# Sums over partitions of twelve modulation blocks, and two gate rows, by DMA and VectorE instead of by TensorE

## What is computed

```python
mod = jnp.dot(jax.nn.silu(c), w_ada) + b_ada            # c: 1 x 1024, w_ada: 1024 x 6144
shift1, scale1, gate1, shift2, scale2, gate2 = jnp.split(mod, 6, axis=-1)
h = _rmsnorm(x, norm1_w) * (1.0 + scale1) + shift1      # input of the mixer (stage 6)
x = x + gate1 * jnp.dot(merged, w_out)
h2 = _rmsnorm(x, norm2_w) * (1.0 + scale2) + shift2     # input of the last FFN (stage 7)
x = x + gate2 * ffn
```

## Time and profile before

| | |
|---|---|
| time, median of 3 runs | 1506.94 us (1505.27 to 1507.37) |
| the profiled execution | 1505.48 us |
| its span, first to last instruction | 1503.7 us |
| granted TensorE clock, mean | 0.992 |
| busy: PE / DVE / ACT / POOL | 1450.5 / 951.1 / 713.1 / 161.4 us |
| instructions: PE / DVE / ACT / POOL | 6819 / 1315 / 1034 / 260 |
| DMA | 279.15 MB, 201717 packets, 186 GB/s on average |

### The profile page before, as it was taken

The page is one execution under the profiler, slowest core; times in us unless marked ns, Lnnn a source line. Parts: engine busy times, 40 slices in busy tenths (PEclk is TensorE's granted clock), DMA queues, the critical chain, the costliest instruction groups (busy, mean ns, idle before and its releaser), DMA issues.

```text
span 1503.7 us, 17990 instructions
## 1 busy us (share of the span) xinstructions
PE 1450.5 (96%) x6819; PEld 1194.5 (79%) x6819; DVE 951.1 (63%) x1315; ACT 713.1 (47%) x1034; POOL 161.4 (11%) x260
## 2 busy tenths in 40 slices
PE   7999999999999999999899999998999999799997
PEld 6888878778888888888788788886877787688886
DVE  5666557677566576565777766655668576555553
ACT  5444355455444354443654544443655643354441
POOL 0800010000000010000252100000542110000000
PEclk9999999999999999999999999999999999899999
DMA  8866746147667666665542586643645354375551
GB/s 262 265 196 230 239 141 209 36 141 228 222 222 245 217 196 216 220 237 189 172 140 91 169 257 219 231 168 119 211 157 193 119 184 150 108 223 169 185 194 56
DMA packets 201717, 279.15 MB, mean 186 GB/s; under 512 B 8804, under 2 KB 126096, under 8 KB 201632
## 3 DMA queue, kind: packets, MB, share of 16 engines
q1 hardware_dynamic: 201376, 277.90, 56.0%
q10 hardware_dynamic: 256, 0.11, 0.0%
HBM read 276.93 MB, written 1.05 MB: 185 GB/s over the span
## 4 chain that ended last, share of the span: by engine, by line
PE 90%; DVE 4%; ACT 3%; issue 2%; POOL 1%; DMA 0%; ACTq 0%; DVEq 0%; POOLq 0%
PE ps L529 27%; PE ps L532 27%; PE ps L530 27%; PE ps L802 2%; PE ps L1038 1%; PE ps L691 1%; PE ps L1319 1%; ACT junk L633 1%; PE ps L481 1%; ACT xh L720 1%; DVE wlo L450 1%; DVE xtmp L1624 1%; ACT whi L441 1%; DVE xtmp L710 0%; POOL st L642 0%
## 5 line engine op out<-in xcount | busy, mean ns | idle before, releaser
L450 DVE TENSOR_TENSOR wlo<-raw,whi 128x1024 fp32r<-128x1024 f32 (+2 forms) x474 | 565.4, 1223 | 201.2 <-ACT whi L441 200.8
L529 PE MATMUL ps<-whi,xh 128*128 128x512 f32 (+2 forms) x1440 | 573.0, 398 | 19.0 <-ACT xh L720 12.4
L530 PE MATMUL ps<-wlo,xh 128*128 128x512 f32 (+2 forms) x1440 | 558.7, 388 | 0.0
L532 PE MATMUL ps<-whi,xl 128*128 128x512 f32 (+2 forms) x1440 | 551.4, 388 | 0.8 <-DVE xl L715 0.7
L441 ACT ACTIVATE whi<-raw 128x1024 fp32r<-128x1024 f32 (+2 forms) x474 | 469.3, 1043 | 166.9 <-PE ps L532 153.6
L529 PEld LDWEIGHTS ps<-whi,xh 128*128 128x128 f32 x1440 | 273.2, 190 | 76.9 <-issue 19.1
L532 PEld LDWEIGHTS ps<-whi,xl 128*128 128x128 f32 x1440 | 272.7, 189 | 58.1 <-DVE xl L715 1.6
L530 PEld LDWEIGHTS ps<-wlo,xh 128*128 128x128 f32 x1440 | 273.7, 190 | 51.8 <-issue 0.2
L529 PE MATMUL ps<-whi,gh 128*128 128x512 f32 x440 | 172.9, 393 | 0.0
L530 PE MATMUL ps<-wlo,gh 128*128 128x512 f32 x440 | 171.3, 389 | 0.0
L532 PE MATMUL ps<-whi,gl 128*128 128x512 f32 x440 | 153.5, 389 | 0.0
(11 more groups left out here) (241 smaller groups left out, 962.5 us busy)
## 6 DMA issues: line engine op xcount, KB each, us to landing
raw<-in_ffn_w_in_dram SPq DMA_DIRECT2D x174, 512.0 KB, 5.1
raw<-in_ffn_w_out_dram SPq DMA_DIRECT2D x40, 1024.0 KB, 5.2
raw<-in_w_in_dram SPq DMA_DIRECT2D x26, 1024.0 KB, 5.0
adat<-in_w_ada_dram SPq DMA_DIRECT2D x96, 256.0 KB, 5.5
raw<-in_w_ffn_gate_dram SPq DMA_DIRECT2D x22, 512.0 KB, 4.1
raw<-in_w_ffn_up_dram SPq DMA_DIRECT2D x22, 512.0 KB, 5.2
raw<-in_hyb_w_in_dram SPq DMA_DIRECT2D x10, 1024.0 KB, 5.1
raw<-in_gla_w_in_dram SPq DMA_DIRECT2D x10, 1024.0 KB, 5.1
```

Source lines behind the costliest of these rows:

```text
L450: e.tensor_tensor(split_of(wlo, j), raw_of(j), split_of(whi, j).bitcast(F32), ALU.subtract).then_inc(*wlo_made.up(j))
L529: e.matmul(ps[:, 0:n], a, whi_of(j, k), start=first and k == 0, stop=False)
L530: last = e.matmul(ps[:, 0:n], a, wlo_of(j, k), start=False, stop=False)
L532: last = e.matmul(ps[:, 0:n], b, whi_of(j, k), start=False, stop=final and k == subs[j][2] - 1)
```

## The change

TensorE, and with it PSUM, has no part in the modulation vectors any more.

- A sum over partitions. Behind unit `ada_units[10c + 11]` SP sends `adaacc` to memory in four DMAs (pieces of 32 values, so that each 128 x 512 tile lies there regrouped), and behind unit `ada_units[10c + 12]` it reads it back in four DMAs into an `adat` buffer as a ninth tile (c, 8): partition j of a group of 32 now holds four rows of 128 values. VectorE (`ada_sum`) adds the four in two steps, transposes in blocks of 32 x 32, reduces over 32 columns, and adds the bias.
- Tiles are now added behind the last split of the unit after their own (`ada_tiles.get(u - 1)`), where it was the unit before. The rule for loading stays: a tile's load waits until the tile before last, in the order of loads (`ada_order`), is done; the ninth tiles count in that order.
- `ada_add` with k = 0 waits until the block before has been sent.
- Gate rows. SP writes eight columns of `modc` to memory (behind units U0[5] + 10 and U0[6] + 8), and loads them as rows, behind U0[6] + 10 and U0[7] + 4, as the gains are loaded. The diagonals, the matmuls and the copies go.

The diff, without the lines that only declare signals or remove calls:

```diff
-        ada_at = {ada_units[10 * c + k]: (c, k) for c in range(12) for k in range(8)}
+        ada_tiles, ada_sent, ada_n = {}, {}, {}
+        for i, u in enumerate(ada_units):
+            ada_tiles[u] = [(i // 10, i % 10)] if i < 120 and i % 10 < 8 else []
+            if i >= 12 and i % 10 == 2:
+                ada_tiles[u].append((i // 10 - 1, 8))
+            if i >= 11 and i % 10 == 1:
+                ada_sent[u] = i // 10 - 1
+            for tile in ada_tiles[u]:
+                ada_n[tile] = len(ada_n)
+        ada_order = list(ada_n)
+        ada_out = nc.dram_tensor("ada_out", [12, P, 512], F32, kind="Internal").ap()
+        gate_rows = nc.dram_tensor("gate_rows", [2, D], F32, kind="Internal").ap()
...
-                if j == last_sub[u] and ada_tile(u, -1):
-                    ada_add(e, *ada_tile(u, -1))
+                if j == last_sub[u]:
+                    for c, k in ada_tiles.get(u - 1, []):
+                        if k < 8:
+                            ada_add(e, c, k)
+                        else:
+                            ada_sum(e, c)
...
+        def ada_sum(e, c):
+            n = ada_n[c, 8]
+            z = adat[n % 2]
+            e.wait_ge(*s_ada[n % 2].at(n))
+            e.tensor_tensor(z[:, 0:256], z[:, 0:256], z[:, 256:512], ALU.add).then_inc(*ada_step.up(c, 0))
+            e.wait_ge(*ada_step.at(c, 0))
+            e.tensor_tensor(z[:, 0:P], z[:, 0:P], z[:, P:256], ALU.add).then_inc(*ada_step.up(c, 1))
+            e.wait_ge(*ada_step.at(c, 1))
+            e.transpose(z[:, 256:384], z[:, 0:P]).then_inc(*ada_step.up(c, 2))
+            e.wait_ge(*ada_step.at(c, 2))
+            e.tensor_reduce(modc[:, 4 * c:4 * c + 4], z[:, 256:384].rearrange("p (b n) -> p b n", b=4), AX.X, ALU.add
+                            ).then_inc(*ada_added.up(c, 8))
+            e.wait_ge(*ada_added.at(c, 8))
+            e.tensor_tensor(modc[:, 4 * c:4 * c + 4], modc[:, 4 * c:4 * c + 4],
+                            vcol[:, VR["ba"] + 4 * c:VR["ba"] + 4 * c + 4], ALU.add).then_inc(*mod_made.up(c))
+
+        def load_ada(e, u):
+            for c, k in ada_tiles.get(u, []):
+                n = ada_n[c, k]
+                if n >= 2:
+                    e.wait_ge(*ada_added.at(*ada_order[n - 2]))
+                if k < 8:
+                    e.dma_start(adat[n % 2][:, :], ada_view[:, k, c * 512:(c + 1) * 512]).then_inc(*s_ada[n % 2].up(n))
+                    continue
+                e.wait_ge(*s_sent.at(c))
+                for q in range(4):
+                    e.dma_start(adat[n % 2][32 * q:32 * (q + 1), :].rearrange("p (r n) -> p r n", r=4),
+                                ada_out[c, :, q * P:(q + 1) * P].rearrange("(r p) n -> p r n", r=4)
+                                ).then_inc(*s_ada[n % 2].up(n))
+            if u in ada_sent:
+                c = ada_sent[u]
+                e.wait_ge(*ada_added.at(c, 7))
+                for b in range(4):
+                    e.dma_start(ada_out[c].rearrange("p (q b n) -> b p q n", q=4, b=4)[b],
+                                adaacc[:, b * P:(b + 1) * P].rearrange("p (q n) -> p q n", q=4)).then_inc(*s_sent.up(c))
...
+                if u in (U0[5] + 10, U0[6] + 8):
+                    i, which = (0, 2) if u < U0[6] else (1, 5)
+                    e.wait_ge(*mod_made.at(2 * which + 1))
+                    e.dma_start(gate_rows[i].rearrange("(b p) -> p b", p=P), modc[:, which * 8:which * 8 + 8],
+                                allow_slow_non_contiguous=True).then_inc(*s_gates.up(which))
+                if u == U0[6] + 10:
+                    load_row(e, "g2", gate_rows[0], D, [s_gates.at(2), f_scaled.at(5, 1, 1)])
+                if u == U0[7] + 4:
+                    load_row(e, "g5", gate_rows[1], D, [s_gates.at(5), gr_made.at(1, 1)])
```

More of the change, by code:

```diff
@@ L473, in pe_begin @@
                 pe_vectors(e, (1, 2))
-            if j in ada_sum_at:
-                c = ada_sum_at[j]
-                ps = tb.next(("ada", c), (mod_made, c))
-                for done in tb.freed:
-                    e.wait_ge(*done)
-                e.wait_ge(*ada_added.at(8 * c + 7))
-                for i in range(4):
-                    last = e.matmul(ps[:, i:i + 1], adaacc[:, i * P:(i + 1) * P], ones[:, 0:1], start=i == 0,
-                                    stop=True, skip_group_check=True)
-                last.then_inc(*ada_summed.up(c))
         def dve_begin(e, j):
@@ L835, in at @@
                     pe_hid(e, st, 10)
-                if st == 7 and i == 7:
-                    pe_gate(e, 5)
             def readers(tok, n):
@@ L859, in act_ffn @@
                     act_ghi(e, st, 10)
-                if st == 7 and i == 7:
-                    act_gate(e, 5)
         def dve_ffn(e, st):
@@ L878, in dve_ffn @@
                     dve_glo(e, st, 10)
-                if st == 7 and i == 5:
-                    dve_gate_diag(e, 5)
         hyb_gate = sig("hyb_gate")
@@ L1655, in dve_ada_open @@
                     dve_residual_gate(e, 6, tok, 2)
-                if tok:
-                    for i in range(4):
-                        dve_mod(e, j0 + i)
                 dve_ada_x(e, st, tok)
@@ L1669, in pool_ada_open @@
                 pool_rstd(e, ("h", st, tok))
[L1671 to L1694 removed]
         def dve_residual_gate(e, st, tok, which):
[L1697 removed]
+            name = "g2" if which == 2 else "g5"
+            row = rows[row_slot[name]]
+            if tok == 0:
+                e.wait_ge(*s_row[row_slot[name]].at(name))
             j0, nk = (JO, 8) if st == 6 else (J0[7] + 44, 22)
@@ L2409, in sp_program @@
                     load_row(e, 0, gains[0], D, [])
[L2410 to L2415 removed]
+                load_ada(e, u)
                 if u - 4 in U0:
```

69 lines of the change are left out of this document (10 added, 59 removed).

## The result

The changed kernel takes **1570.87 us** (median of 4 runs, 1567.01 to 1572.12), the one before beside it 1507.15 us (1505.27 to 1507.88): ratio **1.0419, 95% interval 1.0403 to 1.0435**. It is slower by 64 us, where 33 were forecast; the time is 2.9 us above the upper end of the range. The profiled execution has a span of 1565.2 us at a granted clock of 0.970 (before: 1503.7 us).

What follows compares the result with a forecast made beforehand. TensorE, busy 96% of the span, was taken to bound the kernel. From 1505.5 us, 14.2 of TensorE work was subtracted and 48.8 of serial-load delays added: 1540.1 us, range 1510 to 1568.

Steps and rivals of the forecast that it cites:

- The mechanism: At the ninth tiles SP waits for shared buffers, so splits and raw loads alternate in series; 48.8 us over twelve sums.
- What goes from TensorE: Twelve modulation sums, 10.8 us, and two gate row pairs, 3.4 us, leave TensorE: 14.2 us, all on the chain.
- The first serial leg: After a sum unit's split: addition 0.7 us, four read issues 1.7, then the next raw load about 5.8 to its use.
- The sends: Four DMAs of 128-byte pieces per block hold the queue about 8 us, perhaps 16, and stay hidden before the next split.
- rival C: Small packets hold the queue past 15 us; at 20 us a send, 55 us more: 1595 us. Chance 0.06.
- The stage ends: Late raw loads delay the squares that start the next stage: 8.7 us after stage 0, 6.5 after stage 3.
- 2.9 us late: Inside the first product, the split two units after a sum unit ends at 609.0, TensorE wants it at 606.1; 2.9 each.
- The second leg's load: The raw load two units after the sum unit, with a 256 KB tile ahead of it, lands 5.7 us later.
- Load u+3 ... follows in time: The raw load three units after the sum unit waits only for the sum, so it adds no delay.
- c = 4 and the end of stage 2: In mid-down, copies run 16 us ahead of TensorE, more than the 11 us two serial loads lose; cost 0.
- A: The existing room covers all load delays, so only the 14.2 us gain shows: 1491 us. Chance 0.12.
- B: Serial legs are half to one microsecond shorter; stage ends and the opening remain, 15 to 25 us: 1506 to 1516. Chance 0.12.

Runs made afterwards that it cites:

- Run 1: Changed kernel with a third adat buffer that only the ninth tiles use: 1502.82 us, ratio 0.9979 to the kernel before.
- run 2: Changed kernel with tiles added behind the split of the unit before their own, as before the change, block sent and summed earlier: 1491.7 us, ratio 0.9905.
- run 7: Kernel before the change, with tiles added and summed on TensorE two units later and nothing else: 1509.09 us, ratio 1.0013.
- run 13: Changed kernel without its 48 sends, the reads taking weights from memory instead: 1569.56 us, ratio 1.0408.
- run 14: run 2 with each block sent and read in one DMA of 2 KB pieces, sums not the reference's: 1492.94 us, ratio 0.9906.
- run 10: run 3 plus four reads per block, sized and placed as in the changed kernel, into a buffer nobody uses: 1562.65 us, ratio 1.0370.
- run 16: run 10 with the next block's tile 3 issued behind SP's second wait, ahead of the raw load, as in the changed kernel: 1581.03 us, ratio 1.0493.
- run 11: Changed kernel with SP, at the second unit behind a read, waiting for that unit's load to land before issuing the next: 1572.08 us, ratio 1.0436.
- run 6: Changed kernel with the first gate row's write five units later, at U0[5] + 15 instead of U0[5] + 10: 1570.46 us, ratio 1.0423.
- run 9: Changed kernel without its four reads per block, VectorE summing whatever is in the buffer: 1542.31 us, ratio 1.0241.
- run 4: Changed kernel with each block sent and read in one DMA of 2 KB pieces, sums not the reference's: 1549.2 us, ratio 1.0283.
- run 3: Kernel before the change, with tiles added and summed two units later and two SP waits per block, no transfers added: 1530.44 us, ratio 1.0160.
- run 5: Changed kernel with 3 to 7 matmuls of constants on TensorE before its waits at c = 2, 3, 5, 6, 9, 10: 1568.37 us, ratio 1.0413.
- run 15: run 3 with the next block's tile 3 issued behind SP's second wait, ahead of the raw load: 1544.45 us, ratio 1.0258.

## Why the prediction was right in kind and too small

**Right, by its own steps.**
- The mechanism. Run 1 and run 2 each take away one half of it, the shared buffer or the lag, and all but a few us of the loss are gone; run 7 shows that one half alone costs 2 us.
- What goes from TensorE: 14.2 us forecast; run 2 gives 15 with 3 either way, though one of the twelve sums (c = 2) brought nothing.
- The first serial leg. At c = 6 the addition to the reads, four issues and the load took 0.78, 1.80 and 5.42 us, for 0.7, 1.8 and 5.8 forecast; at the five regular places the load took 5.4 to 5.9.
- VectorE's part: 1.61 us per sum (133.55 to 135.16 for c = 0) for 1.8, and free.
- The sends: hidden (runs 13 and 14). The forecast had up to 16 us per send by the rule of the Trainium skill (DMA: Bandwidth & Descriptors, "Specifications"), and 20 in rival C; had the sends held up the loads, run 13 would have brought that back. Here the sends' 128-byte pieces cost nothing that shows in the time, so that rule leaves no mark here; that a 64 KB send lands in 4.8 us and a 64 KB read in 512-byte rows in 1.9 is what the trace has of it.
- The stage ends: c = 8 7.4 us for 6.5, c = 1 10.5 for 8.7.

**Wrong, by the term.** The places cost 73.6 us for 48.8, and the opening of stage 6 another 2.3. The profiled execution asks for 75.7 (61.5 more than before, and the 14.2 gained), the medians for 78.
- *The wait taken as the cost.* This is the largest error. The seven waits for a split at c = 2, 3, 5, 6, 9 and 10 are 4.71, 3.87, 4.85 and 3.05, 3.19, 6.92 and 3.66 us long, 30.3 in all; the same places cost 44.6 us. The step that failed is "2.9 us late", taken as a cost of 2.9: each such wait cost 1.5 to 3.0 us more than itself (c = 6: 4.8 for 3.19; c = 10: 5.2 for 3.66; c = 2: 7.7 for 4.71), 14.3 in all. The forecast had no term for the clock. Of the matmuls of L558, L559 and L561, 52 start 0.41 to 0.45 us behind the one ahead, instead of 0.23, just after these seven waits: 10.4 us. In the whole trace there are 144, where the kernel before has 56: 88 x 0.2 = 17.6 us. The other 3.9 us at the seven waits are not broken down.
- *The second leg's load.* The forecast took 5.7 us "(256 KB ahead of it)". At c = 2, 3, 6, 9 and 10 it took 8.20, 6.92, 6.67, 8.96 and 6.32, in the mean 7.4; at the second place of c = 5 6.7. The step that failed is the one that added 0.2 us to a row of a pair of loads with nothing ahead of it. In the changed kernel there is the tile ahead (5.5 us without it, 7.3 with it, at c = 2 of runs 10 and 16), another tile and load u+3 behind (run 11, at c = 2 and 9), and at c = 9 the gate's 1024 pieces (8.96 us with them, 8.00 without, run 6). "Load u+3 ... follows in time" was looked at for its own lateness only, not for what it takes from u+2. The loads are 9.6 us longer than forecast in all, the waits behind them only 5.1 (30.3 for 25.2), since other steps of the legs were shorter than forecast (at c = 6 the first load 5.42 for 5.8, the addition and the tile's issue 1.1 for 1.3).
- *c = 4 and the end of stage 2.* Forecast 0, measured 4.6 us. The loads of the down product, two deep there, fell behind (ScalarE waits up to 9.5 us for them), so the squares that open the next stage came late. The seven split buffers were counted as cover for one loss, and they did not suffice; no run tests this place by itself. Eleven of the slow matmuls stand at the opening behind it, where the kernel before has none: 2.2 us of the 4.6 are the clock.

From 48.8 to 73.6 this is 14.3 beyond the waits, 5.1 in the waits, 4.6 at c = 4, and 0.8 at c = 0, 1, 7 and 8 together. The gate write, forecast at 1.0, took about 1.0 at its place (run 6).

**The range.** "About 0.7 us either way" per serial leg held for the first legs (loads of 5.4 to 6.0 us for 5.8) and missed that the errors of the second legs and of the clock are on one side: each stands for traffic or for a state that a row taken from a quiet stretch doesn't have. The range's upper end was drawn for reads that are slow to issue, which they were not (1.8 us for 1.7); that the time is no more than 2.9 us above it is luck. The rivals A and B, with shorter legs, had 0.24 of the chance, one with longer legs and a clock that falls had none of its own.

**What stays open.** The 6 us of run 9 near the end of stage 2. Why a second leg's load still takes some 6.7 us with load u+3 held back (run 11). How the 22 us that large pieces save in the series (run 4) divide between three issues fewer (1.8 us down to one issue, per block) and longer rows. And why the clock fell at the opening of stage 6 in run 2 and not in the kernel before, with the same 1.8 us of idle time; in run 14, which is run 2 with larger pieces, it did not fall either (1.78 us idle, then a granted clock of 1.00), so this need not belong to the change.

## What to carry to other kernels

Before work is moved to a queue of loads, count its buffers per period: here a ninth tile in two buffers whose release lags by two units turned three-deep loads into a series, and one more buffer or an addition two units earlier turned 1.042 into 0.998 and 0.990. Take a transfer's length from a row with the same traffic ahead of it and behind it, since a load that is on the edge shares the engines with all that SP issues next. And price a wait of TensorE as the wait plus what the granted clock loses behind it, here 1.5 to 3.0 us for waits of 3 us and more.

## What the runs showed of the hardware that I had not expected

- Two idle times of TensorE of 1.77 and 1.78 us at the same point of the program were followed by a granted clock of 0.50 in one kernel and 1.00 in the other (run 2 and before).
- TensorE's waits for a split of 2.0 to 2.8 us went either way. There are 22 of them in runs 1, 3, 4, 5, 9, 10, 11, 13 and 15: in the 3 us behind 15 of them the granted clock was 0.50 to 0.73, behind the other seven 1.00. Waits of 2.25 us did both, in runs 10 and 15.
- Behind the waits of 3 to 7 us in the changed kernel the clock stood at 0.5 for 2.9 to 5.9 us; behind 1.11 us at c = 6 of run 5 it stayed at 1.00.
- One DMA of 4 KB in 4-byte pieces took 12.5 us to land and cost the kernel about 1 to 5 by its place; without 48 DMAs of 64 KB in 128-byte pieces, 4.8 us each, it was 1.3 us faster, which is within the spread of its runs.
